# Mixer A's projections of head pairs 1 to 7 by 2x2 block products, in a hybrid two-layer trunk

## What is computed

```python
def hybrid_layer(x, norm_g, w_in, rel_bias, sinks, w_out, cos, sin):
    h = rmsnorm(x, norm_g)
    proj = jnp.einsum('bsd,de->bse', h, w_in)                # 2048 -> 4*1024 + 2*1024 + 2*128
    aq, ak, av, ag, bq, bk, bv, bg = jnp.split(proj, SPLITS, axis=-1)
    ya = chunk_relbias_attention(aq, ak, av, rel_bias) * silu(ag)   # 16 heads of 64, 512 tokens
    yb = swa_sink_gqa(rope(bq), rope(bk), bv, sinks) * silu(bg)     # window of 2 chunks of 64
    return x + jnp.einsum('bse,ed->bsd', concat([ya, yb]), w_out)

def reference(x, ...):
    for l in range(2):
        x = hybrid_layer(x, ...)
    return rmsnorm(x, final_norm_g)
```

## Time and profile before

| | before |
|---|---|
| median of 3 runs | 1624.91 us |
| lowest, highest | 1624.51, 1634.66 us |
| span of the profiled execution (first to last instruction) | 1622.9 us |
| what lies around the span | about 2 us (1624.91 - 1622.9) |
| granted clock of TensorE, mean | 0.998 of 2.4 GHz |

### The profile page before, as it was taken

How to read it: one execution, slowest core, us unless ns; L and a number is a source line. 1 busy time by engine, 2 the same in 40 slices (tenths; PEclk the granted TensorE clock), 3 DMA queues, 4 the chain that set the end, 5 groups by cost and what they waited for, 6 DMA issues and landing times.

```text
span 1622.9 us, 24332 instructions
## 1 busy us (share of the span) xinstructions
PE 1612.2 (99%) x8249; PEld 1372.5 (85%) x8249; DVE 1126.2 (69%) x2563; ACT 879.3 (54%) x1911; POOL 100.2 (6%) x74
## 2 busy tenths in 40 slices
PE   9999999999999999999999999999999999999997
PEld 8888888888888888899988888888888888888997
DVE  7666665566577877888855665666567677788875
ACT  7555555555646666433455555555546466654333
POOL 0000000000121200010000000000002211000000
PEclk9999999999999999999999999999999999999999
DMA  7232222231322322344442232222232323223443
GB/s 253 90 102 104 77 90 90 90 115 58 120 94 91 97 106 91 103 152 155 162 142 79 90 112 93 85 83 90 93 112 74 115 91 100 96 91 117 130 143 117
DMA packets 50014, 174.30 MB, mean 107 GB/s; under 512 B 6496, under 2 KB 10880, under 8 KB 35984
## 3 DMA queue, kind: packets, MB, share of 16 engines
q1 hardware_dynamic: 49472, 172.69, 31.4%
q10 hardware_dynamic: 432, 0.55, 0.1%
q0 software_dynamic: 32, 0.08, 0.0%
HBM read 160.10 MB, written 8.47 MB: 104 GB/s over the span
## 4 chain that ended last, share of the span: by engine, by line
PE 97%; DVE 2%; DMA 1%; issue 0%; SPq 0%; ACT 0%; DVEq 0%
PE ps_proj L605 23%; PE ps_proj L604 23%; PE ps_proj L603 23%; PE ps_t L660 2%; PE ps_o L673 2%; PE ps_s L651 1%; PE ps_s L652 1%; PE ps_o L715 1%; PE ps_s L690 1%; PE ps_o L603 1%; PE ps_o L605 1%; PE ps_o L604 1%; PE ps_t L701 1%; PE ps_o L831 1%; PE ps_proj L831 1%; PE ps_o L827 1%
## 5 line engine op out<-in xcount | busy, mean ns | idle before, releaser
L603 PE MATMUL ps_proj<-act_hi,w_hi 128*128 128x512 f32 x1632 | 642.2, 394 | 0.0
L605 PE MATMUL ps_proj<-act_hi,w_lo 128*128 128x512 f32 x1632 | 638.1, 391 | 0.0
L604 PE MATMUL ps_proj<-act_lo,w_hi 128*128 128x512 f32 x1632 | 637.2, 390 | 0.0
L1313 DVE TENSOR_TENSOR w_lo<-w_raw,w_hi 128x512 fp32r<-128x512 f32 (+1 forms) x528 | 382.7, 740 | 128.7 <-ACT w_hi L925 124.8
L925 ACT ACTIVATE w_hi<-w_raw 128x512 fp32r<-128x512 f32 (+1 forms) x528 | 336.6, 656 | 181.4 <-DVE w_raw L1627 58.3
L605 PEld LDWEIGHTS ps_proj<-act_hi,w_lo 128*128 128x128 f32 x1632 | 306.3, 188 | 66.0
L603 PEld LDWEIGHTS ps_proj<-act_hi,w_hi 128*128 128x128 f32 x1632 | 306.7, 188 | 58.3
L604 PEld LDWEIGHTS ps_proj<-act_lo,w_hi 128*128 128x128 f32 x1632 | 306.8, 188 | 57.8
L925 ACT ACTIVATE probs<-probs,rden 128x128 f32<-128x128 f32 (+3 forms) x128 | 72.1, 563 | 119.2 <-DVE rden L1406 119.2
L991 ACT ACTIVATE probs<-probs,nmax 128x128 f32<-128x128 f32 (+3 forms) x128 | 71.9, 562 | 93.9 <-DVE nmax L1385 90.9
L1313 DVE TENSOR_TENSOR arena<-ps_t,arena 128x512 fp32r<-128x512 f32 (+4 forms) x168 | 85.1, 510 | 43.4 <-ACT arena L925 42.6
(11 more groups left out here) (294 smaller groups left out, 2287.2 us busy)
## 6 DMA issues: line engine op xcount, KB each, us to landing
w_raw<-w SPq DMA_DIRECT2D x107, 1024.0 KB, 4.8
w_raw<-w SPq DMA_DIRECT2D x98, 256.0 KB, 3.6
temp<-temp SPq DMA_DIRECT2D x72, 64.0 KB, 4.1
strips_tables<-ext SPq DMA_DIRECT2D x16, 256.0 KB, 5.8
temp<-xT SPq DMA_DIRECT2D x16, 256.0 KB, 4.2
xs<-xy SPq DMA_DIRECT2D x16, 256.0 KB, 4.3
temp<-xs SPq DMA_DIRECT2D x16, 256.0 KB, 4.0
strips_tables<-ext SPq DMA_DIRECT2D x16, 224.0 KB, 5.7
```

Source lines behind the costliest of these rows:

```text
L603: pe.matmul(dst, wh, act_hi[:, k, :], start=start, stop=False)
L604: pe.matmul(dst, wh, act_lo[:, k, :], start=False, stop=False)
L605: return pe.matmul(dst, wl, act_hi[:, k, :], start=False, stop=stop)
L1313: return nc.vector.tensor_tensor(dst, src, hi, ALU.subtract)
```

## The change

Units u = 1 to 7 project q and k as one pair of tiles (points 0 to 7) and gate and v as another (points 8 to 15). Of the 8 pairs of k rows of a pair of tiles four go by block products and four as before. The 8 chunks of a pair of tiles are, in order, plain, four with seven blocks each, three plain (`IN_CHUNKS`). A block chunk is 21 matmuls of 128x256. The two accumulators of a pair take two banks and its four other products two more: `ps_proj` and the second banks of scores and transposes, with the roles swapped for the second pair. So mixer A's scores and transposes have one bank each, and wait for step e-1 in place of e-2.

VectorE: `lo_in` splits chunk p + 3, `sum_w_in` makes the four weight sums of chunk p + 4 when that has seven blocks (p = 0, 5, 6, 7, 8, 13, 14, 15), `sum_of_products_in` comes at points 6 and 14, `take_pair` (two additions and two scalings) at point 8 and after point 15. ScalarE: `hi_in` of chunk p + 3, `copy_p1` at points 6 and 14. In each layer's head ScalarE scales eight rows of x (`scale_h`), GpSimd forms the sums of h over them (`sum_h`), and both splitting engines split these (`hi_h_sums`, `lo_h_sums`). The sums lie where rows of `xy` were, so finished rows of mixer A go to DRAM (`keep_y`) and come back before the output projection. The host lays the weights of the pairs out in blocks. Cut to its core:

```diff
+IN_SUM_K = 4
+IN_CHUNKS = (("p", 0), ("s", 0), ("s", 1), ("s", 2), ("s", 3), ("p", 1), ("p", 2), ("p", 3))
+AHEAD = 3
+SUM_AT = 6
...
+        def in_banks(pair):
+            x, y = (ps_proj[0], ps_proj[1]), (ps_s[1], ps_t[1])
+            return (y, x) if pair else (x, y)
...
             def scores_a(g, v, e0, e):
-                if e >= 2:
-                    pe.wait_ge(biased, e0 + (e - 1))
+                if e >= 1:
+                    pe.wait_ge(biased, e0 + e)
...
-                dst = ps_s[e % 2][:, 0:n]
+                dst = ps_s[0][:, 0:n]
...
             def turn_a(e0, e):
-                if e >= 2:
-                    pe.wait_ge(pt_done, e0 + (e - 1))
+                if e >= 1:
+                    pe.wait_ge(pt_done, e0 + e)
...
+            def unit_sums(T, L, u, att):
+                for p in range(16):
+                    attend(att, p)
+                    if p == 1:
+                        turn_v(T)
+                    i = p % 8
+                    kind, n = IN_CHUNKS[i]
+                    q = pair_in(L, u, p)
+                    if i == 0:
+                        pe.wait_ge(in_summed, q * 4 + 4)
+                    if i == 1:
+                        pe.wait_ge(rows_added, q * 2 + (2 * L + 2))
+                    pe.wait_ge(w_lo_done, T * PTS + (p + 1))
+                    if kind == "s":
+                        sum_products_in(L, p // 8, i, n)
+                    else:
+                        plain_products_in(p // 8, i, n)
...
+            def hi_in(T, L, u, j):
+                if kind == "s":
+                    act.wait_ge(in_wsum, (pair_in(L, u, j) * IN_SUM_K + (n + 1)) * 4)
+                else:
+                    act.wait_ge(in_raw[IN_PLACE[i]], raw_count(L, u, j))
+                in_passed(act, L, u, j - 4)
+                copy(hi_f[:, in_place(i)], raw_f[:, in_place(i)]).then_inc(w_hi_done, 1)
...
+            def sum_w_in(L, u, j):
+                dve.wait_ge(in_raw[IN_PLACE[i]], raw_count(L, u, j))
+                nc.vector.tensor_tensor(b[S1], b[S3], b[W22], ALU.add).then_inc(in_wsum, 1)
+                dve.wait_ge(in_wsum, done + 1)
+                nc.vector.tensor_tensor(b[S2], b[S1], b[W11], ALU.subtract).then_inc(in_wsum, 1)
+                nc.vector.tensor_tensor(b[S3], b[W11], b[S3], ALU.subtract).then_inc(in_wsum, 1)
+                dve.wait_ge(in_wsum, done + 3)
+                nc.vector.tensor_tensor(b[S4], b[W12], b[S2], ALU.subtract).then_inc(in_wsum, 1)
...
+            def sum_of_products_in(L, u, p):
+                dve.wait_ge(in_copied, q + 1)
+                nc.vector.tensor_tensor(w2r, p6, w1l, ALU.add).then_inc(in_summed, 1)
+                dve.wait_ge(in_summed, done + 1)
+                nc.vector.tensor_tensor(w2l, p7, w2r, ALU.add).then_inc(in_summed, 1)
+                nc.vector.tensor_tensor(w1r, p5, w2r, ALU.add).then_inc(in_summed, 1)
+                dve.wait_ge(in_summed, done + 3)
+                nc.vector.tensor_tensor(w2r, p5, w2l, ALU.add).then_inc(in_summed, 1)
...
+            def take_pair(T, L, u, pair, dsts):
+                dve.wait_ge(proj_done, T + (2 * pair + 3))
+                for bank_of, row, (dst, scale) in rows:
+                    nc.vector.tensor_tensor(dst, bank_of[:, :], row, ALU.add).then_inc(rows_added, 1)
+                for n, (bank_of, row, (dst, scale)) in enumerate(rows):
+                    dve.wait_ge(rows_added, q * 2 + (2 * L + n + 3))
+                    nc.vector.scalar_tensor_tensor(out=dst, in0=dst, scalar=scale, in1=rstd[:, :], op0=ALU.mult, op1=ALU.mult
+                                                   ).then_inc(proj_free, 1)
...
+            def unit_sums(T, L, u, att, ab, g, v):
+                for p in range(16):
+                    def other():
+                        if isinstance(u, int) and p + AHEAD >= 16:
+                            lo_next(tile0(L) + A_SLOTS, p + AHEAD - 16)
+                        else:
+                            lo_in(T, p + AHEAD)
+                        j = p + AHEAD + 1
+                        if IN_CHUNKS[j % 8][0] == "s" and not (isinstance(u, int) and j >= 16):
+                            sum_w_in(L, u, j)
...
+                    attend(att, p, L, ab, Y_STAGE, other)
+                    if p == 1:
+                        lo_v_a(att[1])
+                    if p == 2:
+                        gate(att[0])
+                    if p % 8 == SUM_AT:
+                        sum_of_products_in(L, u, p)
+                    if p == 8:
+                        take_pair(T, L, u, 0, ((t_q, 1.0), (t_k, 1.0)))
+                    if p == 9:
+                        lo_q(g)
+                    if p == 13:
+                        lo_k(v)
+                take_pair(T, L, u, 1, ((t_graw, 0.5), (t_v, 1.0)))
```

More of the change, by code:

```diff
@@ L203, in trunk @@
         presum = sem("presum")
+        in_raw = [sem(f"in_raw{i}") for i in range(len(IN_FIRST))]
+        in_done = sem("in_done")
+        in_wsum = sem("in_wsum")
+        in_copied = sem("in_copied")
+        in_summed = sem("in_summed")
+        rows_added = sem("rows_added")
+        h_scaled = sem("h_scaled")
+        h_summed = sem("h_summed")
+        h_sum_hi = sem("h_sum_hi")
+        h_sum_lo = sem("h_sum_lo")
+        y_kept = sem("y_kept")
+        y_back = sem("y_back")
         first_done = sem("first_done")
@@ L551, in _ @@
                 prefetch(T, 1)
-                for s in range(2, 4):
-                    prefetch(T, s)
+                for j in range(4):
+                    load_in(T, L, 1, j)
                 with sp.If(L > 0):
@@ L746, in unit, with sum_products_in @@
                         project(T, s, pt)
+            def sum_products_in(L, pair, i, n):
+                (c1, c2), (pa, pb) = in_banks(pair)
+                (c11, c12), (c21, _) = left_right(c1), left_right(c2)
+                (p1, p6), (p5, p7) = left_right(pa), left_right(pb)
+                h_hi = [left_right(act_hi[:, 2 * n + r, :]) for r in range(2)]
+                h_lo = [left_right(act_lo[:, 2 * n + r, :]) for r in range(2)]
+                t_hi = [left_right(h_sum(0, 2 * n + r)) for r in range(2)]
+                t_lo = [left_right(h_sum(1, 2 * n + r)) for r in range(2)]
+                pe.wait_ge(h_sum_lo, (L * IN_SUM_K + n + 1) * 2)
+                products = ((c11, W12, h_hi[1][0], h_lo[1][0]), (c12, S4, h_hi[1][1], h_lo[1][1]),
+                            (c21, W22, t_hi[1][0], t_lo[1][0]), (p1, W11, h_hi[0][0], h_lo[0][0]),
+                            (p5, S1, t_hi[0][0], t_lo[0][0]), (p6, S2, t_hi[1][1], t_lo[1][1]),
+                            (p7, S3, t_hi[0][1], t_lo[0][1]))
+                for dst, b, hi, lo in products:
+                    first = n == 0 and b in (W11, S1)
+                    last = n == IN_SUM_K - 1 and dst not in (c11, c12, c21)
+                    wh = in_block(hi_f, i, b)
+                    pe.matmul(dst, wh, hi, start=first, stop=False, skip_group_check=True)
+                    pe.matmul(dst, wh, lo, start=False, stop=False, skip_group_check=True)
+                    mm = pe.matmul(dst, in_block(lo_f, i, b), hi, start=False, stop=last, skip_group_check=True)
+                mm.then_inc(in_done, 1)
@@ new lines, in plain_products_in @@
+            def plain_products_in(pair, i, j):
+                (c1, c2), _ = in_banks(pair)
+                first = in_place(i).start
+                for r, dst in enumerate((c1[:, :], c2[:, :])):
+                    for k in range(2):
+                        row = 2 * IN_SUM_K + 2 * j + k
+                        cols = slice(first + (2 * r + k) * P, first + (2 * r + k + 1) * P)
+                        last = j == KT // 2 - IN_SUM_K - 1 and k == 1
+                        pe.matmul(dst, hi_f[:, cols], act_hi[:, row, :], start=j == 0 and k == 0, stop=False, skip_group_check=True)
+                        pe.matmul(dst, hi_f[:, cols], act_lo[:, row, :], start=False, stop=False, skip_group_check=True)
+                        mm = pe.matmul(dst, lo_f[:, cols], act_hi[:, row, :], start=False, stop=last, skip_group_check=True)
+                if last:
+                    mm.then_inc(proj_done, 2)
+                else:
+                    mm.then_inc(in_done, 1)
@@ L1924, in _ @@
             with pool.Fori(0, DEPTH) as L:
+                for n in range(IN_SUM_K):
+                    sum_h(L, n)
                 B = tile0(L) + A_SLOTS
@@ L1957, in tile_columns @@
     for u in range(PAIRS):
-        cols += [base + u * P for base in (ag, aq, ak, av)]
+        cols += [base + u * P for base in (aq, ak, ag, av)]
     cols += [bk, bq, bq + P, bv]
```

246 lines of the change are left out of this document (205 added, 41 removed).

## The result

| | before | after |
|---|---|---|
| median | 1624.71 us (4 runs) | 1875.64 us (4 runs) |
| lowest, highest | 1624.12, 1634.66 us | 1875.21, 1877.02 us |
| span of the profiled execution | 1622.9 us | 1873.4 us |
| granted clock of TensorE, mean | 0.998 | 0.954 |

The changed kernel takes 1.1538 times as long, interval 1.1506 to 1.157: 251 us more. The forecast was 1797 us with a range up to 1850. The direction and the main mechanism (a loop over two engines that TensorE can no longer hide) were right. The size was not, and the prediction had put at nothing what the lower clock costs.

The account below looks back on a forecast made before the run. The prediction took TensorE's matmuls as the present bound, hiding a loop of VectorE and ScalarE that the change lengthens. It summed 1624.9 + 165 (units) + 10 (heads) - 2.6 (units behind the seven) = 1797 us, range 1730 to 1850.

Parts of the forecast that it names:

- TensorE's saving: Two pairs of tiles per unit: narrow matmuls take 1.6 to 2.8 us per unit off TensorE, 22 to 39 over 14 units.
- VectorE's load: Per unit: 17.3 us of added work make VectorE busy 48.3 us, as long as TensorE needs.
- First half: Points 0 to 7 of a unit: the loop of 24.2 us gains 9.5 and becomes 33.7 us.
- the walk: Tracing a unit's queues step by step with their waits: VectorE ends at 64.2 us; 63.0 was taken.
- Middle: Point 8: work ahead of the first pair's additions takes 5.3 us, so TensorE starts point 9 at 39.0 us.
- Second half: From point 9: TensorE needs 19.5 us plus 2.4, to 60.9; VectorE with waits ends at 64.2; taken 63.0.
- rival (C): TensorE also drops to its lower clock level in the units: 35 us more, about 1840 to 1870 us; chance 0.12.
- The head: Last four tiles of each layer's head: VectorE 4.9 us late, 9.8 in all; ScalarE's scalings and GpSimd's sums at 0.
- the unit behind the seven: After each layer's seven units: it starts with TensorE further ahead and wins 1.3 us per layer.
- (A): Units: TensorE stays the bound, ready work fills idle time, a unit takes 48.4 to 49.6 us, 1594 us; chance 0.05.
- (B): Units: VectorE is the bound but half its waits vanish, a unit of 56 to 58 us, 1714 us; chance 0.13.
- (D): The change does not bring the fewer matmuls it claims; given no chance.

Follow-up runs that it names:

- busy_middle: The changed kernel with 30 extra 128x512 matmuls per unit at points 8 and 9 that only keep TensorE busy: 1847.9 us, ratio 1.1376.
- busy_front: The changed kernel with 19 extra 128x512 matmuls per unit at points 1 to 3 that only keep TensorE busy: 1875.5 us.
- no_h_sums: The changed kernel without GpSimd's 16 subtractions per layer that form the sums of h: 1872.7 us.
- head_bare: The changed kernel without GpSimd's 16 subtractions per layer and without ScalarE's eight scalings in each head: 1868.4 us.
- both_ahead: The changed kernel with VectorE's weight sums ahead of its split and ScalarE's copy ahead of its exp: 1782.9 us, ratio 1.0975.

## Why the prediction was wrong in size

By the first biases of the units the 250.5 us of span (1873.4 - 1622.9) divide into: units, 2 x 7 of them, 229.5 (67.6 against 51.2 each); head of layer 0, 11.1; the stretch between the two layers' units, 8.6; the tail, 1.4. The forecast had 165, 4.9, 3.6 and -1.3.

**TensorE's saving: right, at the low end.** At the upper level narrow matmuls start 0.12 us apart and wide ones 0.2275 (36 from 186.59 to 194.78), so that a unit saves 2 x (10.92 - 10.06) = 1.7 us of the 1.6 to 2.8 forecast. From 173.59 to the end of its last chunk at 194.78 TensorE needed 21.2 us, of which 1.7 are the lower clock (`busy_middle`, above), so 19.5; forecast 19.5.

**VectorE's load: right.** 48.3 us per unit forecast, 47.3 measured.

**First half: 33.7 us forecast, 35.1 measured in the unit shown** (to the inverted sum that starts at 167.84), 34.5 in five of the seven units of layer 0. The walk struck out VectorE's waits for TensorE's scores, since these came from TensorE's pace before. They came back, 0.41 + 0.60 + 0.92 us at 148.31, 151.54 and 155.90. TensorE's rows ahead of the third:

```profile
153.93 1.20 PE L777 MATMUL ps_o<-arena,v_st 128*128 128x512 f32 x6
...
155.12 0.42 PE L755 MATMUL ps_s<-k_st,arena 128*128 128x384 f32 x1
```

TensorE has no idle time from 142.83 to 161.5: it reaches the scores late because a whole chunk, and at point 6 the V products too, stand ahead of them in its queue, as before the change (1.99 us there). In a unit of `busy_front` the first two waits are gone and the third is 0.68, so the low clock has a part in them. It is a small one over all units: the waits for line 756 are 19.5 us there in all and 20.3 in the changed kernel.

**Middle: 39.0 forecast for TensorE's point 9, 173.59 - 132.84 = 40.8 measured** (40.1 in five of the seven units), most of the excess inherited from the first half.

**Second half.** The waits of the walk were there: 2.95 us at point 11 (about 2 forecast), 1.80 at point 13 (1.8). One of 1.17 us for the split of point 10 was not foreseen; it is gone in `busy_middle`. The first step that failed is the sentence behind them: the walk gave 64.2 us, TensorE alone 60.9, and I took 63.0, on the ground that the queue is in order. That ground speaks for the walk's full 64.2. Choosing below it cost 1.2 us per unit, 17 in all. The units of `busy_middle`, without the low clock in the middle, take 65.5 on average.

**The clock: the second step that failed, and the largest term.** I had rival (C) as a separate case with a chance of 0.12, when my own walk already contained its condition: two idle stretches of 2 to 3 us around points 8 and 9. It should have been a term of the forecast, where it stood at nothing. As a rival its size was nearly right, 35 us estimated, 27.8 measured by `busy_middle`, and so was its picture of two low stretches per unit of which one costs nothing. A low stretch is shorter than it assumed: 1.7 us lost in the middle, not a whole chunk's 2.5. The fall of the clock in the units is also one of the signs by which the prediction was to be called wrong. The Trainium skill (TensorE: Matmul & The Clock Gate, HAM oscillation) tells of a matmul stream with recurring waits, for DMAs there, that falls to the lower clock each time anew. The trace agrees, though the waits here are for VectorE: 0.92 in the unit, and two falls in the unit shown.

**The head: the third.** Without the scalings and GpSimd's sums the head is still 6.0 us longer, where 4.9 were forecast for VectorE's work. ScalarE's scalings, taken at 0 with an end of 5, cost 3.5 in layer 0: the cover I had named, a late VectorE, was itself waiting for ScalarE. GpSimd's sums, taken at 0, cost about 1.5 net. Where the cover of an edit is an engine that is itself on the path, the cover is none. In layer 1 `no_h_sums` shortened the stretch between the units by 2.1 us and `head_bare` by no more than that; the other 6.5 us there were not taken apart. About 2 of them are the unit behind the seven, which was to gain 1.3 us and lost 2 instead: its step 4 comes 14.87 us after its first bias (553.97 - 539.10), before 12.91 (426.23 - 413.32). Behind layer 1 the same unit lost as much, and the whole tail 1.4.

Together: 17 (63.0 for 64.2), 28 (clock), 19 (the rest of the units, by difference: 14 x 16.4 - 165 - 17 - 28; 1.0 us per unit in the first half, 0.3 in the middle), 6 (head of layer 0), 5 (between the layers), 3 (tail) make the 78 us between forecast and result.

**The rivals.** (A) did not happen: VectorE's waits per unit are 20 us, not under 1. (B), a unit of 56 to 58 us, did not happen either, and the better order alone did not reach it: units of 61 us in `both_ahead`. With the sums on GpSimd they are 55, but then VectorE has less to do than (B) assumed. (D) had no ground. Of what would show the forecast true, VectorE's 48 us per unit, the mixed chain and TensorE's waits are there; TensorE is busy in 80% of a unit (54.11 of 67.85), but in 89% of the span, where the prediction had 80%. What the change could have won at best, 1.7 us per unit or 24 in all, was small against what it put on the other two engines. Even without the weight sums and with the better order the kernel is 66 us slower than before.

What stays open: whether `both_ahead` with fillers in the middle alone would get its share of the clock back; it wasn't tried. Its one unit at 1.00 takes 59.7 us where the seven of layer 0 take 60.9 on average, so an estimate is 14 x 1.2 = 17 us at most. Nor was the changed kernel with its splits four chunks ahead, as before, in place of three, so what the shorter lead costs is not known.

## What to carry to other kernels

Before moving work onto an engine that is idle for 40% of the time, look at what its idle time is made of: where it is a loop with another engine, most of what is added inside the loop is paid (5.7 of 8.5 us here). Within such a loop put what depends on nothing first, on both engines: two swapped pairs of instructions were worth 93 us. And when a walk shows TensorE idle again and again, the lower clock belongs in the forecast, priced at the places where TensorE is the late engine.
